# Two rounded matmul passes for every small sum of squares, in a planned encoder kernel on one core

## What is computed

```python
h = rms_norm(x, norm_w)
(aq, ak, av, ag, bq, bk, bv, bg, cq, ckv, ckr, cg, du, dg) = split(h @ w_in)   # 5824 columns
# A: differential attention, 4 heads; q and k normed by rms_norm, rotary on a quarter; output rms_norm (subln)
# B: grouped-query attention, 4 query heads, 2 key heads, q and k normed, 2-D rotary
# C: latent attention: rms_norm of cq and ckv, up-projections w_uq, w_ukv, q and k normed, shared rotary key ckr
# D: pooled windows 2/4/8/16 minus the token, a matmul per group
y = concat(A * silu(ag), B * silu(bg), C * silu(cg), D * silu(dg))
x = x + y @ w_out
def rms_norm(x, w):
    return x * rsqrt(mean(x * x, axis=-1) + 1e-6) * w
```

## Time and profile before

| what | value |
|---|---|
| median of 3 runs | 924.63 us (924.15, 924.63, 1456.06) |
| profiled execution, its own time | 924.1 us |
| its span | 922.3 us, so 1.8 us lie outside it |
| TensorE matmuls | 904.1 us busy, 7054 recorded |
| VectorE / ScalarE | 636.8 us / 585.9 us busy |

### The profile page before, as it was taken

The page is one execution under the profiler, slowest core; times in us unless marked ns, Lnnn a source line. Parts: engine busy times, 40 slices in busy tenths (PEclk is TensorE's granted clock), DMA queues, the critical chain, the costliest instruction groups (busy, mean ns, idle before and its releaser), DMA issues.

```text
span 922.3 us, 18111 instructions
## 1 busy us (share of the span) xinstructions
PE 904.1 (98%) x7054; PEld 861.0 (93%) x7054; DVE 636.8 (69%) x1071; ACT 585.9 (64%) x1045; POOL 0.2 (0%) x4
## 2 busy tenths in 40 slices
PE   8989999999999999999999999999999999999998
PEld 7988998998989999999999989999989998999998
DVE  7785897768777776576665658876687667666552
ACT  7677766677666666655554678566686666665331
POOL 0000000000000000000000000000000000000000
PEclk9999999999999999999999999999999999999999
DMA  8644333342334343345444444334425434435552
GB/s 329 256 163 158 137 138 128 138 134 106 140 138 140 138 157 113 138 174 192 165 174 178 181 144 177 125 108 172 146 94 182 136 139 162 150 122 190 201 190 85
DMA packets 22997, 143.83 MB, mean 156 GB/s; under 512 B 2560, under 2 KB 4736, under 8 KB 6528
## 3 DMA queue, kind: packets, MB, share of 16 engines
q1 hardware_dynamic: 22768, 142.64, 43.2%
q10 hardware_dynamic: 144, 0.04, 0.0%
HBM read 140.57 MB, written 2.10 MB: 155 GB/s over the span
## 4 chain that ended last, share of the span: by engine, by line
PE 75%; ACT 11%; DVE 10%; issue 2%; DMA 1%; SPq 0%; ACTq 0%; DVEq 0%
PE dense L721 21%; PE dense L723 21%; PE dense L722 21%; DVE w_lo L1315 4%; ACT w_hi L1010 4%; PE s_ps L885 4%; PE o_ps L920 3%; PE t_ps L901 1%; PE norm_ps L841 1%; ACT y_hi L1139 1%; ACT c_st L1150 1%; DMA raw<-w_stream_dram 1%; ACT c_st L1149 1%; ACT c_st L1151 1%; ACT row L1035 1%
## 5 line engine op out<-in xcount | busy, mean ns | idle before, releaser
L721 PE MATMUL dense<-h_hi,w_hi 128*128 128x272 f32 (+1 forms) x1440 | 427.7, 297 | 4.2 <-ACT row L1035 2.9
L723 PE MATMUL dense<-h_hi,w_lo 128*128 128x272 f32 (+1 forms) x1440 | 413.3, 287 | 0.0
L722 PE MATMUL dense<-h_lo,w_hi 128*128 128x272 f32 (+1 forms) x1440 | 411.5, 286 | 0.0
L1315 DVE TENSOR_TENSOR w_lo<-raw,w_hi 128x1024 fp32r<-128x1024 f32 (+1 forms) x257 | 313.3, 1219 | 104.7 <-ACT w_hi L1010 98.3
L1010 ACT ACTIVATE w_hi<-raw 128x1024 fp32r<-128x1024 f32 (+1 forms) x257 | 271.3, 1056 | 63.6 <-PE dense L723 51.2
L721 PEld LDWEIGHTS dense<-h_hi,w_hi 128*128 128x128 f32 x1440 | 271.3, 188 | 11.2 <-issue 6.7
L722 PEld LDWEIGHTS dense<-h_lo,w_hi 128*128 128x128 f32 x1440 | 271.6, 189 | 1.3
L723 PEld LDWEIGHTS dense<-h_hi,w_lo 128*128 128x128 f32 x1440 | 271.0, 188 | 0.0
L721 PE MATMUL dense<-y_hi,w_hi 128*128 128x272 f32 (+1 forms) x500 | 144.0, 288 | 5.8 <-ACT q_st L1055 2.2
L723 PE MATMUL dense<-y_hi,w_lo 128*128 128x272 f32 (+1 forms) x500 | 142.7, 285 | 0.0
L722 PE MATMUL dense<-y_lo,w_hi 128*128 128x272 f32 (+1 forms) x500 | 142.4, 285 | 0.0
(11 more groups left out here) (161 smaller groups left out, 838.7 us busy)
## 6 DMA issues: line engine op xcount, KB each, us to landing
raw<-w_stream_dram SPq DMA_DIRECT2D x128, 1024.0 KB, 4.8
out_dram<-x SPq DMA_DIRECT2D x8, 256.0 KB, 6.6
x<-xt_dram SPq DMA_DIRECT2D x3, 544.0 KB, 9.2
raw<-w_stream_dram SPq DMA_DIRECT2D x3, 512.0 KB, 7.7
con<-consts_dram SPq DMA_DIRECT2D x1, 984.0 KB, 7.4
x<-xt_dram SPq DMA_DIRECT2D x2, 272.0 KB, 4.8
raw<-w_stream_dram SPq DMA_DIRECT2D x2, 256.0 KB, 4.4
d_w<-consts_dram SPq DMA_DIRECT2D x2, 256.0 KB, 5.1
```

Source lines behind the costliest of these rows:

```text
L721: nc.tensor.matmul(ps, whi, xhi, start=first, stop=False)
L722: nc.tensor.matmul(ps, whi, xlo, start=False, stop=False)
L723: return nc.tensor.matmul(ps, wlo, xhi, start=False, stop=last)
L1315: signal(nc.vector.tensor_tensor(w_lo[:, g % RING, 0:n], raw[:, e % RAW, CHUNK * half:CHUNK * half + n], w_hi[:, g % RING, 0:n].bitcast(F3 ...
```

## The change

Each of the 48 small sums of squares (36 `rope_stat`, 4 `lat_stat`, 8 `sub_stat`) is computed as the sum of two rounded matmuls: the squares are rounded into `sq_hi`, the rest goes into `sq_lo`, and a rounded table of ones is multiplied with each. For the 22 single heads and the 8 sub-norms ScalarE makes `sq_hi` (one more copy) and a new VectorE stage `sq_low` makes `sq_lo`. For the 14 two-tile heads and 4 latent sums VectorE makes both, in `sq_sum`. The sum over the whole input stays a float32 matmul.

Beside it the plan moves. `y_split`, which stood early in a slot, stands after the `lift` and, on VectorE, after the `split`; VectorE's `gate` stands ahead of its `split`; the first lift of pair 3 stands ahead of `lat_fin` of `ckv`; `kr` goes four slots later, one gate two. In layer 1 the latent query tiles are computed for 256 and the pooling tiles for 264 of 272 tokens. Small tiles are packed together (`stat` holds the exponents' bias, lambda and the constants).

```diff
-GATE_LATER = {("cg", 0): 5, ("cg", 1): 4, ("cg", 2): 0, ("cg", 3): 2, ("ag", 0): 0, ("ag", 1): 2, ("ag", 2): 2,
+GATE_LATER = {("cg", 0): 5, ("cg", 1): 6, ("cg", 2): 0, ("cg", 3): 2, ("ag", 0): 0, ("ag", 1): 2, ("ag", 2): 2,
...
-                 y_split=0.205, xscale=0.283, sub_pre=0.439, x_out=0.55, p_out=0.56, gate=0.65, s_exp=0.579,
-                 lift=0.6, up_out=0.705, split=0.71, x_square=0.72, y_gate=0.23, lam_exp=0.793, v_out=1.297)
-AT_VECTOR = dict(sq_sum=0.2, rope_mid=0.25, s_max=-0.418, lam_dot=-0.35, sub_fin=-0.345, rope_fin=-0.34, lat_fin=0.055, head_out=0.17,
-                 y_split=0.19, pool=0.266, xscale=0.283, gate=0.72, s_scale=0.491, x_out=0.512, rescale=0.55,
+                 y_split=0.66, xscale=0.283, sub_pre=0.439, x_out=0.55, p_out=0.56, gate=0.65, s_exp=0.579,
+                 lift=0.6, up_out=0.705, split=0.71, x_square=0.72, y_gate=0.73, y_lat=0.72, lam_exp=0.793, v_out=1.297)
+AT_VECTOR = dict(sq_sum=0.2, sq_low=0.2, rope_mid=0.25, s_max=-0.418, lam_dot=-0.35, sub_fin=-0.345, rope_fin=-0.34, lat_fin=0.055, head_out=0.17,
+                 y_split=0.75, pool=0.266, xscale=0.283, gate=0.7, s_scale=0.491, x_out=0.512, rescale=0.55,
...
+MOVED = {**{("lift", l, 3, 0): -0.55 for l in range(DEPTH)},
...
-        at(s + 4, ("rope_pre", l, "kr", 0, None))
-        at(s + 5, ("rope_stat", l, "kr", 0))
-        at(s + 6, ("rope_fin", l, "kr", 0))
+        at(s + 8, ("rope_pre", l, "kr", 0, None))
+        at(s + 8, ("sq_low", "rope", l, "kr", 0))
+        at(s + 9, ("rope_stat", l, "kr", 0))
+        at(s + 10, ("rope_fin", l, "kr", 0))
...
+        if kind == "du":
+            return first_query(l) // 2
+        return first_query(l) if kind in ("aq", "bq", "cq", "ag", "bg", "cg", "dg") or (kind, j) == ("cqr", 0) else 0
...
+        def two(ps, table, hi, lo):
+
+            nc.tensor.matmul(ps, table, hi, start=True, stop=False)
+            return nc.tensor.matmul(ps, table, lo, start=False, stop=True)
...
-            if key in PAIRED:
-                pe.wait_ge(summed, sum_no[("rope", l, key, i)])
-            else:
-                pe.wait_ge(pre_done, pre_no[("rope_pre", l, key, i)])
+            pe.wait_ge(summed, sum_no[("rope", l, key, i)])
...
-            square = nc.scalar.activation(sq[:, 2 * half, t0:L], src, ACT.Square)
-            if branch:
-                link(square)
-                square = nc.scalar.activation(qw[:, half, t0:L], src, ACT.Copy, scale=pcol(l, key))
-            signal(square, pre_done, pre_no[("rope_pre", l, key, i)])
+            link(nc.scalar.activation(sq[:, 2 * half, t0:L], src, ACT.Square))
+            link(nc.scalar.activation(qw[:, half, t0:L], src, ACT.Copy, scale=pcol(l, key)))
+            signal(nc.scalar.activation(sq_hi[:, half, t0:L], sq[:, 2 * half, t0:L], ACT.Copy),
+                   pre_done, pre_no[("rope_pre", l, key, i)])
...
+            a, b = sq[:, first, t0:L], sq[:, first + 1, t0:L]
+            link(nc.vector.tensor_tensor(a, a, b, ALU.add))
+            high = sq_hi[:, half, t0:L]
+            link(nc.vector.tensor_copy(high, a))
+            signal(nc.vector.tensor_tensor(sq_lo[:, half, t0:L], a, high.bitcast(F32), ALU.subtract), summed, n)
+
+        def sq_low(what, *of):
...
+            dve.wait_ge(pre_done, pre_no[(("rope_pre" if what == "rope" else "sub_pre"), *of)])
+            half = parity(*stage)
+            signal(nc.vector.tensor_tensor(sq_lo[:, half, t0:L], sq[:, 2 * half, t0:L],
+                                           sq_hi[:, half, t0:L].bitcast(F32), ALU.subtract), summed,
+                   sum_no[(what, *of)])
```

More of the change, by code:

```diff
@@ L141, in at @@
     def at(slot, stage):
-        kind = "y_gate" if stage[:2] == ("y_split", "gate") else stage[0]
+        kind = {"gate": "y_gate", "lat_fin": "y_lat"}.get(stage[1], "y_split") if stage[0] == "y_split" else stage[0]
         if kind in at_engine:
@@ L214, in make_plan @@
             at(s, ("rope_pre", l, key, i, None))
-            if key in PAIRED:
-                at(s, ("sq_sum", "rope", l, key, i))
+            at(s, ("sq_sum" if key in PAIRED else "sq_low", "rope", l, key, i))
             at(s + 1, ("rope_stat", l, key, i))
@@ L236, in make_plan @@
                 at(s, ("sub_pre", l, n))
+                at(s, ("sq_low", "sub", l, n))
                 at(s, ("sub_stat", l, n))
@@ L835, in rope_stat @@
             t0 = rope_from(l, key)
-            if key in PAIRED:
-                pe.wait_ge(summed, sum_no[("rope", l, key, i)])
-            else:
-                pe.wait_ge(pre_done, pre_no[("rope_pre", l, key, i)])
+            pe.wait_ge(summed, sum_no[("rope", l, key, i)])
             norm_free("rope_stat", l, key, i)
-            sums = nc.tensor.matmul(norm_ps[:, t0:L], halves, sq[:, 2 * parity("rope_stat", l, key, i), t0:L],
-                                    start=True, stop=True)
+            half = parity("rope_stat", l, key, i)
+            sums = two(norm_ps[:, t0:L], halves_r, sq_hi[:, half, t0:L], sq_lo[:, half, t0:L])
             sums.then_inc(stat_done, 1)
@@ L847, in lat_stat @@
             norm_free("lat_stat", l, key)
-            nc.tensor.matmul(norm_ps[:, 0:L], ones, sq[:, 0 if key == "cq" else 1, :],
-                             start=True, stop=True).then_inc(stat_done, 1)
+            if (l, key) == (0, "cq"):
+                pe.wait_ge(ones_ready, 1)
+            half = parity("lat_stat", l, key)
+            two(norm_ps[:, 0:L], ones_r, sq_hi[:, half, :], sq_lo[:, half, :]).then_inc(stat_done, 1)
         def v_turn(l, kind, i, j):
@@ L924, in sub_stat @@
         def sub_stat(l, n):
-            pe.wait_ge(pre_done, pre_no[("sub_pre", l, n)])
+            pe.wait_ge(summed, sum_no[("sub", l, n)])
             norm_free("sub_stat", l, n)
             t0 = first_query(l)
-            nc.tensor.matmul(norm_ps[:, t0:L], ones, sq[:, 2 * parity("sub_stat", l, n), t0:L],
-                             start=True, stop=True).then_inc(stat_done, 1)
+            half = parity("sub_stat", l, n)
+            two(norm_ps[:, t0:L], ones_r, sq_hi[:, half, t0:L], sq_lo[:, half, t0:L]).then_inc(stat_done, 1)
         run = dict(setup=warm_up, chunk=chunk, xsum=xsum, rope_stat=rope_stat, lat_stat=lat_stat, v_turn=v_turn, mix=mix,
@@ L1092, in lat_pre @@
                 act.wait_ge(summed, sum_no[("lat", l, "cq")])
-            first = 0 if key == "cq" else 1
+            first = 0 if key == "cq" else 2
             signal(nc.scalar.activation(sq[:, first:first + n, :], c_st[:, k0:k0 + n, :], ACT.Square), pre_done,
```

77 lines of the change are left out of this document (41 added, 36 removed).

## The result

The changed kernel takes 934.13 us (933.24 to 935.19, 4 runs) beside 924.56 us of the kernel before: the ratio is 1.0106, with a 95% interval of [1.0086, 1.0125]. That lies within 2%, but above my range of 911 to 929, and on the other side of no change than my 922.0. One of the four runs of the kernel before took 1456.06 us; it counts in the median and not in the ratio. The profiled execution took 933.24 us, with a span of 931.5.

The account below looks back on a forecast made before the run. Bound by TensorE's number of matmuls, so only fewer or narrower matmuls or fewer waits help. 924.1 - 4.8 - 1.8 - 2.3 - 4.3 + 11.1 = 922.0 us; range for 8 in 10: 911 to 929.

Parts of the forecast that it names:

- Step 1: Sums of squares on TensorE: two rounded matmuls at 0.252 us replace 0.454; 24 sums not awaited save 4.8 us.
- Step 2: Narrower tiles in layer 1: 144 matmuls lose 16 columns and 192 lose 8, saving 1.8 us.
- Steps 3 and 4: Shorter TensorE waits in the latents' chain and up-projection, 2.3 us saved, and at gates and lifts, 4.3 us saved.
- the latents' growth: Latents' chain: a rounding and a subtraction for each of two latent sums on VectorE ahead of `y_lo`, 1.6 us.
- Step 5: TensorE's sums wait for the new operands, mainly `sq_low` behind splits in VectorE's full queue: 11.1 us lost, bounds 4 to 14.
- step 3: Latents and up-projection: earlier lift and split against added VectorE work; 0.7 us less in layer 0, 1.6 in layer 1.
- rival B: ScalarE becomes the late engine: its copies stand ahead of lifts and bank waits return; 928.6 us, chance 0.1.
- A: Earlier gates and lifts pull VectorE's queue forward, so it reaches `sq_low` in time; 913 us, chance 0.25.
- C: Two rounded passes cost what the two float32 records cost, so the sums save nothing; 926.8 us, chance 0.03.
- D: Longer waits drop TensorE's clock; a 24-matmul chunk takes 3 us more after each of three waits; 931 us, chance 0.02.

Follow-up runs that it names:

- e3: The changed kernel with all 48 sums back in float32, keeping the change's moves and narrower tiles: 913.09 us.
- e8: The changed kernel with the 30 single-head and sub-norm sums in float32, but ScalarE still making their rounded copies, which nothing reads: 920.97 us.
- e1: The changed kernel without the 30 VectorE subtractions of single heads and sub-norms; the second rounded pass reads the high part again: 918.67 us.
- e10: The kernel before with only the change's narrower tiles in layer 1; float32 sums, every step at its old place: 922.17 us.
- e2: The changed kernel with the 30 single-head and sub-norm sums back in float32, without their copies and subtractions; pairs and latents keep two passes: 915.21 us.
- e5: The changed kernel with VectorE's subtraction for single heads and sub-norms placed ahead of the split instead of behind it: 923.28 us.

## Why the prediction was wrong

**The bound** was read rightly: TensorE's matmuls, with waits that matter by the place of an instruction in VectorE's queue.

**Step 1** was right in its term: 0.25 for 0.454 us, and 4.8 us for those not awaited. Chunk by chunk, the change gains 5.7 us over e3 at open sums. Not all of that stays: two passes for the 30 singles without their subtraction give 2.5 us net (e8 to e1), where 30 x 0.20 would be 6.0.

**Step 2**, 1.8 us, measured 1.86.

**Steps 3 and 4**, 6.6 us with the latents' growth in them, gave 9.3 with float32 sums. In layer 0 the up-projection starts 0.27 late, where I said 0.3. The gate wait went. Float32 sums don't have that growth, up to 1.7 us by the expectation for e3, so the forecast to set beside the 9.3 is some 8.3. By the starts of chunks, 3.4 of the 9.3 arise in layer 0 and 5.9 in layer 1 (e3 against e10).

**Step 5 failed, and with it the sum.** It had 11.1 us and bounds of 4 to 14. Chunk by chunk the change loses 26.0 us against e3. At my own places:

- Layer 0, key head 1 and the chunks ahead of it: 3.3 us, forecast 2.3. Most of the extra is the split's lateness of 0.9 us, shown above, half of it from the copy and half from the moved `y_split`.
- Layer 0, key head 3's stretch: 3.8, forecast 3.0.
- Layer 1, sub-norm and key head 3: 8.0, forecast 4.0. The waits themselves were well placed (2.98 and 2.42 us, forecast 2.7 and 2.4), and with up to 3.0 us for the lower clock they cover the 8.0. The 0.9 us at the lift between them, which I took off here, go with the moves alone: e3 gains 1.1 us there.
- All other places: some 11, forecast 1.8 beside the latents' growth in step 3. Here the reading failed most: latents and up-projections, value and query heads, sub-norms. I looked for sums whose VectorE queue was full and gave the rest a fraction of a subtraction.

By cause, and with all signs, the sums cost 20.7 us:

| part | us | from |
|---|---|---|
| pairs and latents in two passes | +2.1 | e3 to e2 |
| ScalarE's 30 copies | +6.0 | e2 to e8 |
| two rounded passes for singles, no subtraction | -2.5 | e8 to e1 |
| subtraction, even ahead of the split | +4.8 | e1 to e5 |
| its place behind the split, with the lower clock | +10.3 | e5 to change |

The medians of e1 and e5 lie between runs with and without a stretch at the lower clock. By their runs at 1.000 alone the last three rows are -3.4, +4.9 and +11.1. Of the last, 7.2 us are the waits for `sq_lo` (15.3 to 8.1) and up to 3.0 the clock.

The clearest hole is the second row. Step 5 names 13 us of copies and charges nothing for them: their only way into my sum was rival B, which counted a lift more than 0.6 us late and nothing for what waits on VectorE. At key head 1 the copy delays the exponents, these VectorE's softmax, this the split, and the split `sq_lo`. How the 6.0 us divide over such chains was not traced further. My sum used VectorE's times of before as if nothing upstream had moved.

**Rivals.** A (VectorE not late) is refuted by the wait list. B (ScalarE late, 928.6) has its mechanism in e8, with 6.0 us for the copies. I had made it an alternative to step 5, and they add. C is refuted by the starts at 80.11. D, at 0.02, came true in two places of layer 1 at about half the 3 us I had priced a chunk at. The Trainium skill, TensorE: Matmul & The Clock Gate, section HAM oscillation, which I had cited for D with no row to show it, is borne out in kind: gaps between dense stretches can throttle the array again, here behind waits for VectorE rather than for transfers. Its gaps are waits of 3 to 5 us; here shorter ones did it in the profiled execution, 2.98 and 2.42. Without D the change would be at about 931, still outside the range.
